# Where the split weights and the operands of a float32 block lie in SBUF

## The reference

```python
def first_block(x, ...):
    h = rmsnorm(x, g[0]);  proj = h @ w_in
    # pool mixer, width-3 convolution, attention over the top 64 keys of an index score
    up    = einsum('bsnc,ncd->bsnd', branches, w_branch)
    mixed = sum(sigmoid(h @ w_gate + b_gate) * up, branches) @ w_out
    x = x + rmsnorm(mixed, g[1])
    m = square(relu(rmsnorm(x, g[2]) @ w_up)) @ w_down
    return x + rmsnorm(m, g[3])

def second_block(x, c, ctx, ...):
    # shift, scale, gate = (silu(c) @ w_ada + b_ada) in three parts
    p = modulate(rmsnorm(x)) @ w_in_2         # q, k, v, z_a, u_b, z_b, g_a, g_b
    # attention over x and ctx with rotated q and k; 2-D Fourier mixing of u_b
    y = (sigmoid(g_a) * ((attn * silu(z_a)) @ w_proj_a)
         + sigmoid(g_b) * ((fourier(u_b) * silu(z_b)) @ w_proj_b)) @ w_out_2
    return rmsnorm(x + gate * y)
```

## Time and profile before

| | before |
|---|---|
| median of 3 runs | 2342.02 us (2341.75 to 2343.25) |
| the profiled execution | 2343.5 us, its span 2341.7 us |
| TensorE matmuls | 2312.0 us busy, 99%, 15980 instructions |
| TensorE weight loads | 2152.9 us busy, 92% |
| VectorE | 1469.0 us busy, 63% |
| ScalarE | 1070.9 us busy, 46% |
| DMA | mean 202 GB/s |
| granted TensorE clock | 0.997 of full speed |

### The profile page before, as it was taken

How to read it: one execution, slowest core, us unless ns; L and a number is a source line. 1 busy time by engine, 2 the same in 40 slices (tenths; PEclk the granted TensorE clock), 3 DMA queues, 4 the chain that set the end, 5 groups by cost and what they waited for, 6 DMA issues and landing times.

```text
span 2341.7 us, 37604 instructions
## 1 busy us (share of the span) xinstructions
PE 2312.0 (99%) x15980; PEld 2152.9 (92%) x15980; DVE 1469.0 (63%) x1844; ACT 1070.9 (46%) x1422; POOL 40.4 (2%) x61
## 2 busy tenths in 40 slices
PE   7999999999999999999999999999999999999998
PEld 7989999999999988988988988998899979999986
DVE  6757477777787667544555555555755545676665
ACT  5344435444344456444443443444655545433443
POOL 1000000000000001000000000000100000000000
PEclk9999999999999999999999999999999999999999
DMA  8855676677777765656656556556764444778763
GB/s 268 248 162 157 187 215 218 217 224 233 245 226 254 251 222 172 180 196 190 180 193 194 181 188 204 183 191 195 237 179 144 145 126 127 258 255 266 237 203 139
DMA packets 246368, 473.73 MB, mean 202 GB/s; under 512 B 21166, under 2 KB 25624, under 8 KB 244536
## 3 DMA queue, kind: packets, MB, share of 16 engines
q1 hardware_dynamic: 242888, 454.40, 61.1%
q0 software_dynamic: 3312, 16.92, 2.2%
HBM read 467.05 MB, written 4.21 MB: 201 GB/s over the span
## 4 chain that ended last, share of the span: by engine, by line
PE 97%; DVE 1%; issue 1%; ACT 0%; DMA 0%; SPq 0%; POOL 0%; POOLq 0%; DVEq 0%; ACTq 0%
PE ps L860 20%; PE ps L861 20%; PE ps L862 20%; PE ps L853 10%; PE ps L855 10%; PE ps L854 10%; PE ps L788 1%; PE ps L727 1%; PE ps L623 1%; PE ps L649 1%; PE ps L767 0%; PE ps L768 0%; PE ps L777 0%; PE ps L801 0%; PE ps L664 0%
## 5 line engine op out<-in xcount | busy, mean ns | idle before, releaser
L1220 DVE TENSOR_TENSOR wlo<-raw,whi 128x1024 fp32r<-128x1024 f32 (+1 forms) x768 | 927.5, 1216 | 736.9 <-ACT whi L892 735.7
L892 ACT ACTIVATE whi<-raw 128x1024 fp32r<-128x1024 f32 (+1 forms) x768 | 802.9, 1053 | 962.5 <-PE ps L862 618.2
L860 PE MATMUL ps<-op0h,whi 128*128 128x256 f32 x3248 | 927.7, 286 | 1.1 <-DVE wlo L1220 1.1
L861 PE MATMUL ps<-op0l,whi 128*128 128x256 f32 x3248 | 919.7, 283 | 0.0
L862 PE MATMUL ps<-op0h,wlo 128*128 128x256 f32 x3248 | 919.6, 283 | 0.0
L860 PEld LDWEIGHTS ps<-op0h,whi 128*128 128x128 f32 x3248 | 623.9, 192 | 6.4 <-issue 5.8
L861 PEld LDWEIGHTS ps<-op0l,whi 128*128 128x128 f32 x3248 | 624.1, 192 | 2.0 <-issue 1.4
L862 PEld LDWEIGHTS ps<-op0h,wlo 128*128 128x128 f32 x3248 | 623.9, 192 | 0.0
L853 PE MATMUL ps<-whi,op1h 128*128 128x512 f32 x640 | 249.5, 390 | 0.0
L854 PE MATMUL ps<-wlo,op1h 128*128 128x512 f32 x640 | 249.0, 389 | 0.0
L855 PE MATMUL ps<-whi,op1l 128*128 128x512 f32 x640 | 249.0, 389 | 0.0
(11 more groups left out here) (262 smaller groups left out, 1911.2 us busy)
## 6 DMA issues: line engine op xcount, KB each, us to landing
raw<-in_w_in SPq DMA_DIRECT2D x256, 512.0 KB, 4.2
raw<-in_w_up SPq DMA_DIRECT2D x128, 512.0 KB, 3.7
raw<-in_w_down SPq DMA_DIRECT2D x128, 512.0 KB, 4.0
raw<-in_w_ada SPq DMA_DIRECT2D x96, 512.0 KB, 4.6
raw<-in_w_gate SPq DMA_DIRECT2D x96, 512.0 KB, 4.6
raw<-in_w_out SPq DMA_DIRECT2D x64, 512.0 KB, 4.4
raw<-in_w_branch SPq DMA_DIRECT2D x48, 512.0 KB, 5.0
raw<-in_w_proj_a SPq DMA_DIRECT2D x24, 512.0 KB, 4.2
```

What stands on the lines that cost most here:

```text
L860: pe.matmul(o, wh, xh[:, ka, :], start=first and m % 2 == 0, stop=False, skip_group_check=True)
L861: pe.matmul(o, wh, xl[:, ka, :], start=False, stop=False, skip_group_check=True)
L892: act.activation(whi[q % NSPL][:, :, 0:job.n], raw[i][:, :, 0:job.n], ACT.Copy).then_inc(s_hi, 1)
L1220: v.tensor_tensor(wlo[q % NSPL][:, :, 0:job.n], x, h.bitcast(F32), ALU.subtract).then_inc(s_lo, 1)
```

## The change

Three things move; no instruction, wait or transfer is added or taken away.

1. `line(shift)` moves the allocation on to the next address that is `shift` past a multiple of 256. The split buffers are allocated 64 past such a multiple, and each gets two names for one place: the "T" view begins there, at 64, and the "W" view 64 bytes later, at 128. Each buffer takes 64 bytes more, and with the next `line(64)` its pitch is 4352 bytes instead of 4096.
2. `op0h`, `op0l`, `op1h`, `op1l` lie at 64 past a multiple of 256 instead of 128, and `tmp` behind them follows. `big` is put at 64 past a multiple explicitly, where it lay before; it moves from 154944 to 155200.
3. The row buffer `a5` no longer has a place of its own: it is `tmp[5]`. The small tensors behind it shift.

```diff
         raw = [sb(f"raw{i}", [128, KC, 512]) for i in range(NRAW)]
-        whi = [sb(f"whi{i}", [128, KC, 512], F32R) for i in range(NSPL)]
-        wlo = [sb(f"wlo{i}", [128, KC, 512], F32R) for i in range(NSPL)]
-        op0_at = top[0]
+        def line(shift):
+            top[0] += (shift - top[0]) % 256
+            return top[0]
+
+        def split_buffers(name):
+            w = {"T": [], "W": []}
+            for i in range(NSPL):
+                o = line(64)
+                for mode, shift in (("T", 0), ("W", 64)):
+                    w[mode].append(at(f"{name}{mode}{i}", [128, KC, 512], o + shift, F32R))
+                top[0] = o + 64 + 4 * KC * 512
+            return w
+
+        whi, wlo = split_buffers("whi"), split_buffers("wlo")
+        op0_at = line(64)
         op0h, op0l = sb("op0h", [128, 16, 256], F32R), sb("op0l", [128, 16, 256], F32R)
-        op1_at = top[0]
+        op1_at = line(64)
...
-        a5 = sb("a5", [128, 512])
+        a5 = tmp[5]
...
-        big = top[0]
+        big = line(64)
...
-                h, l = whi[q % NSPL], wlo[q % NSPL]
+                h, l = whi[job.mode][q % NSPL], wlo[job.mode][q % NSPL]
```

More of the change, by code:

```diff
@@ L891, in high @@
                     act.wait_ge(s_pe, q - NSPL + 1)
-                act.activation(whi[q % NSPL][:, :, 0:job.n], raw[i][:, :, 0:job.n], ACT.Copy).then_inc(s_hi, 1)
+                act.activation(whi[job.mode][q % NSPL][:, :, 0:job.n], raw[i][:, :, 0:job.n], ACT.Copy).then_inc(s_hi, 1)
             def square(src, junk, name, tt):
@@ L1217, in low @@
                 job = chunks[q][0]
-                x, h = raw[landed["w", q][0]][:, :, 0:job.n], whi[q % NSPL][:, :, 0:job.n]
+                x, h = raw[landed["w", q][0]][:, :, 0:job.n], whi[job.mode][q % NSPL][:, :, 0:job.n]
                 v.wait_ge(s_hi, q + 1)
-                v.tensor_tensor(wlo[q % NSPL][:, :, 0:job.n], x, h.bitcast(F32), ALU.subtract).then_inc(s_lo, 1)
+                v.tensor_tensor(wlo[job.mode][q % NSPL][:, :, 0:job.n], x, h.bitcast(F32), ALU.subtract).then_inc(s_lo, 1)
             summed = [0, 0]
```

## The result

| | before | after |
|---|---|---|
| median | 2342.3 us (2341.75 to 2343.25, 4 runs) | 2303.3 us (2301.8 to 2307.0, 4 runs) |
| the profiled execution, its span | 2343.5, 2341.7 us | 2307.0, 2305.1 us |

The ratio is 0.9835, with an interval of 0.9818 to 0.9852: 39 us faster. The forecast was 2266, a gain of 76. So the direction held and half of the gain is missing. The time lies in the range, but only just: the range ended at rival 3's 2304. So the first question is whether it was rival 3's mechanism.

What follows compares the result with a forecast made beforehand. TensorE was taken as the bound, 97% of the chain that ended last. 2343.5 - 75.6 (mode W) + 1.0 (breaks) - 1.3 (`mg`, `hc`) = 2267.6; the runs' median 1.5 lower: 2266 us, range 2238 to 2304.

Steps and rivals of the forecast that it cites:

- rival 3: Mode W: bit 8 of the address counts too; even buffers may stay at 120.0 ns, losing half the gain; 2304 us, 9%.
- The bound: TensorE, matmul under way 99% of the span; addresses act only on the step between matmul starts; next bounds charged 0.
- Mode W: 11280 matmuls with `op0`, `op1` get the phases and step of `yah`, 113.3 instead of 120.0 ns: 75.6 us gained.
- nuisance of 1 us: Mode W after breaks: first steps already shorter than 120 ns; an estimated 100 breaks with 10 ns each, 1 us not gained.
- (a): Mode T: how the two streams stand to each other counts; 64/64 stays at 226.7 ns, `mg` and `hc` gain 1.3 us.
- 5.3 ns: Mode T upper bound: 3264 matmuls each lose this if 64/64 is as bad as a 232 ns step; 17.3 us lost.
- A time in proportion to its columns, plus 13.3 ns each: Both modes: a step seems to have the same constant excess at equal phases, whatever the length of the moving stream.
- 1 (moving phase): Mode T: the moving stream's own phase counts, 64 good, 128 bad; another 21.9 us less, 2244 us; 24%.
- 2 (64 over 64 bad for T): Mode W gains, but mode T goes to 228.9 or up to 232 ns: 2273 or 2285 us; 9%.
- 4 (not the phase): Mode W: `yah` is fast through its place as a whole or its shortness; W stays at 120.0 ns, 2342 us; 8%.
- 5: Mode W: as rival 3, but even buffers meet an unseen collision, 13.4 ns over 120.0: 2380 us; 4%.
- The other edits and ScalarE, VectorE: `a5`, `tmp`, `ident`, `ones` at 0, 2 us either way; ScalarE and VectorE, 1059 and 1224 ns a chunk, stay hidden.

Runs made afterwards that it cites:

- experiments 1 to 4: Experiment 1, experiment 2 and the two runs of the map: 2344.8, 2296.8, 2338.0 and 2339.4 us.
- the map: Split buffers dealt out job by job at eight phases, 32 bytes apart, in two kernels with operands at different phases, edited from the changed kernel: 2338.0 and 2339.4 us.
- experiment 1: Changed kernel with the W views put back on the T views, so all phases are equal at 64: 2344.8 us, ratio 1.001.
- experiment 7: Changed kernel with four more transposes of `ident` behind the one-column matmuls at 8 places: 2299.1 us, ratio 0.9812.
- experiments 5: Changed kernel, but the first chunk of 50 mode-W runs reads its weights at 64, equal to the moving phase: 2319.8 us, ratio 0.9901.
- experiment 6: Changed kernel, but the first chunk of 50 mode-W runs takes its split buffers at phase 0, under moving 64: 2288.2 us, ratio 0.9768.
- experiment 8: Changed kernel with the added transposes of experiment 7 and the phase-0 first chunk of experiment 6 at 17 chosen starts: 2279.8 us, ratio 0.9733.
- experiment 2: Changed kernel with the T views moved to 128, where the W views are, operands still at 64: 2296.8 us, ratio 0.9806.

## Why the prediction was right in direction and wrong in size

**The bound.** Right. TensorE sets the time before and after, a change of addresses acts on the step alone, and no other engine or DMA took over: 268 GB/s was the densest slice before, 274 after, and TensorE's waits are unchanged.

**Mode W: this is the step that failed.** "Price: 120.0 - 113.3 = 6.7 ns", for all 11280 matmuls, 75.6 us. The pair of phases was right, and that it gets `yah`'s step is right for 156 of 470 chunks, worth 24.8 us. The other 314 gain 2.2 ns a step, 16.6 us. Over all of them the mean step is 116.3 ns, so by the prediction's own sign, within 1 ns of 113.3, the forecast is wrong. That the time is still inside the range is luck: its upper end was drawn at 2304 for rival 3, whose mechanism isn't at work. The mistake was to take one row for the property of the pair. All four stretches with `yah` in the trace of before were entered in one way: from `op0` over the same weights, at 120.0, with only the moving phase changed. The row could not show that another entry gives another pattern. The shorter steps at the switch back, which I read as a nuisance of 1 us, were perhaps a sign that a step depends on those ahead of it.

**Mode T.** (a), the difference, is right: 226.7 at 64 over 64, `mg` from 228.9 to 226.7, and experiments 1 to 4 show the rule at other phases, but for the second pattern at 192. The 5.3 ns that I charged as the upper bound of a bad pair was not too high: the map has up to 7.5.

**My argument for (a).** "A time in proportion to its columns, plus 13.3 ns each" got the right answer for equal phases and is wrong as a rule: at difference 64 mode W falls by 2 to 7 ns and mode T rises by 6 to 7.

**The rivals.** 1 (moving phase): refuted by experiment 1, W back at 120.0 with the operands at 64. 2 (64 over 64 bad for T): refuted, 226.7. 3 (bit 8, even and odd buffers): its 2304 is the measured time by coincidence. Its mechanism is refuted, since all four buffers are in both patterns, and no buffer stays at 120.0. 4 (not the phase): refuted, no W chunk is at 120.0. 5: refuted with 3. I had no rival with two patterns for one pair of addresses; nothing in one trace would have priced it, but "the price holds only in the context in which the row was taken" would have been a fair case for half of the gain.

**The other edits and ScalarE, VectorE.** Right: nothing (experiment 1); 1056 and 1219 ns a chunk against 1059 and 1224 in the earlier trace rows.

**What the Trainium skill says.** W steps run from 113.3 to 120.3 and T steps from 226.6 to 234.2 ns by address alone. By the Trainium skill, "TensorE: Matmul & The Clock Gate", Part 2, with its two independent read ports, the weight load takes no SBUF read bandwidth from the running matmul. Read as "the two don't act on each other", the trace disagrees, since the step depends on how their two addresses differ. The 16-byte cachelines of the Trainium skill's "SBUF — State Buffer" ("Door 1: The DMA port swizzle") don't predict it either: all phases of the map are multiples of 32, and mode W's step changes from each to the next.

**What stays open.** Why there are two patterns, and what picks one at a break. The distance from a weight load's start to its matmul's start is 110 ns in the fast pattern, 114 to 115 in the slow one and 117 at 120.0, but that says nothing new: in all three the next load starts 2 to 5 ns after the running matmul, so the distance is the step itself less those few ns. The choice isn't fixed by the kind of work in the break: one and the same small step was followed by 113.3 and 117.8 in turn (`bias_flip`), and the added transposes worked at four of seven places. Nor is it fixed by the program (experiment 7). How much it varies between executions of one kernel isn't measured, as each kernel has one trace. The times bound it: those of the kernels with two patterns lie 3 to 6 us apart, which by an estimate from 24 x 4.5 ns a chunk is room for some 30 to 60 chunks at most; experiment 1, where no chunk has a choice, spreads by 5 us too. So the total over many starts holds for each kernel, as the medians of experiments 5, 6 and 8 show, while a single start in a single trace proves little.

## What to carry to other kernels

In a dense run of float32r matmuls with a weight load each, the step depends on how the standing operand's address stands to the moving one's, modulo 256; give each mode its own pair and read the steps from start times, as durations and busy shares don't show 6%. A price read from one stretch holds for the way that stretch was entered: before multiplying it by ten thousand, look for a second stretch that is entered in another way, and if there is none, keep half of the gain in doubt. Where a loop can run in two locked patterns, its start is worth steering: one first chunk with another address moved the time by 17 us one way and 15 us the other (experiments 5 and 6), and with four idle transposes added, 24 us were won on after (experiment 8).

## What the runs showed of the hardware that was not expected

- A pattern, once taken, is kept until something else runs on TensorE: over all ten traces, of the successions from one W(64) chunk to the next without a break 1258 stayed at 113.3 and 1248 at 117.8, and none went over. The longest run, 39 chunks, took 110.5 us at 117.8 in after and 106.4 us at 113.3 in experiment 2.
- How the start led on, by kind (difference 64 behind it), over all traces: T at 226.7, 18 of 18 to 117.8; T at 228.9, 5 of 6 to 113.3; one-column matmuls, 16 of 18 to 117.8, and with the added transposes 10 of 14 to 113.3; a W chunk at 120.0 whose standing phase changes, 50 of 50 to 117.8; one whose moving phase changes, 4 of 4 to 113.3; a W chunk at difference 192, 31 of 50 to 113.3 in experiment 6 and 16 of 17 at the chosen places of 8.
- The two modes want opposite things: W is at its worst at equal phases (120.0, with 160 as bad) and T at its best (226.7).
- Instructions can be added at no cost: with 32 more transposes on the engine that bounds the kernel it is not slower (2299.1 against 2303.3 us, the intervals overlap), and by the trace 80 chunks behind them are faster.
- The same instructions on the same addresses can take either pattern: 2 of the 6 clean run starts ahead of 95 us differ between after and experiment 7.
